# Splitting an output product's and a gate's weights row by row, and an embedding product in three products of parts

## The reference

```python
h = h + jnp.concatenate([att, hm], axis=-1) @ w_out          # "output product", 1024 x 1024
u = rms_norm(h, g_mlp) @ w_ff1                                # 1024 x 4096
h = h + jnp.square(jax.nn.relu(u)) @ w_ff2                    # 4096 x 1024
gate = jax.nn.sigmoid(rms_norm(h, g_ple) @ w_ple_gate + b_ple_gate)
return h + gate * (p_i @ w_ple)                               # p_i: 512 x 256, w_ple: 256 x 1024
```

## Time and profile before

| | |
|---|---|
| runs | 2102.87, 2107.33, 2102.92 us; median 2102.92 |
| profiled execution | 2106.63 us, of which its span 2104.8 us and 1.83 us around it |
| TensorE busy | 2043.9 us, 97% of the span |
| VectorE, ScalarE, GpSimd busy | 1120.6, 864.4, 918.7 us |
| transfers | 194.28 MB, mean 92 GB/s |

### The profile page before, as it was taken

How to read it: one execution, slowest core, us unless ns; L and a number is a source line. 1 busy time by engine, 2 the same in 40 slices (tenths; PEclk the granted TensorE clock), 3 DMA queues, 4 the chain that set the end, 5 groups by cost and what they waited for, 6 DMA issues and landing times.

```text
span 2104.8 us, 26346 instructions
## 1 busy us (share of the span) xinstructions
PE 2043.9 (97%) x10220; PEld 1583.3 (75%) x10220; DVE 1120.6 (53%) x1991; ACT 864.4 (41%) x1373; POOL 918.7 (44%) x1152
## 2 busy tenths in 40 slices
PE   6999999999999999999999999999999999999998
PEld 3877677888888767667888888666766788888867
DVE  5366758986483578944523131446986443123134
ACT  4542434343233557753322222335677432222132
POOL 1344205787575334731655555103455055555530
PEclk9999999999999999999999999999999999999999
DMA  9134631333322310212333322222112133332212
GB/s 320 42 115 143 204 118 41 101 101 100 101 80 87 100 41 21 81 41 81 110 100 100 100 98 83 80 81 66 41 41 81 50 101 101 100 100 84 98 59 100
DMA packets 186668, 194.28 MB, mean 92 GB/s; under 512 B 8496, under 2 KB 181936, under 8 KB 186160
## 3 DMA queue, kind: packets, MB, share of 16 engines
q1 hardware_dynamic: 185968, 189.44, 27.7%
q10 hardware_dynamic: 576, 3.15, 0.4%
HBM read 190.48 MB, written 2.10 MB: 91 GB/s over the span
## 4 chain that ended last, share of the span: by engine, by line
PE 87%; DVE 5%; POOL 3%; ACT 2%; DMA 1%; issue 1%; SPq 0%; ACTq 0%; DVEq 0%; POOLq 0%
PE ps L804 20%; PE ps L806 19%; PE ps L805 19%; PE ps L821 3%; PE ps L823 3%; PE ps L822 3%; PE ps L849 2%; POOL arena_m L2881 2%; PE ps L1256 1%; PE ps L1311 1%; POOL wl L2813 1%; DVE mix L2441 1%; PE ps L1344 1%; PE ps L1363 1%; PE ps L906 1%; PE ps L838 1%
## 5 line engine op out<-in xcount | busy, mean ns | idle before, releaser
L2813 POOL TENSOR_TENSOR wl<-ring,wh 128x256 fp32r<-128x256 f32 x1000 | 748.7, 783 | 853.1 <-ACT wh L1454 852.8
L1454 ACT ACTIVATE wh<-ring 128x1024 fp32r<-128x1024 f32 (+2 forms) x294 | 304.1, 1044 | 326.6 <-PE ps L806 256.2
L804 PE MATMUL ps<-xh,wh 128*128 128x512 f32 (+1 forms) x976 | 383.9, 393 | 3.2 <-POOL wl L2813 2.3
L806 PE MATMUL ps<-xh,wl 128*128 128x512 f32 (+1 forms) x976 | 381.3, 391 | 0.0
L805 PE MATMUL ps<-xl,wh 128*128 128x512 f32 (+1 forms) x976 | 381.2, 391 | 0.0
L804 PE MATMUL ps<-acts,wh 128*128 128x512 f32 x880 | 345.0, 392 | 3.7 <-DVE wl L1974 3.3
L806 PE MATMUL ps<-acts,wl 128*128 128x512 f32 x880 | 342.5, 389 | 0.0
L805 PE MATMUL ps<-acts,wh 128*128 128x512 f32 x880 | 342.4, 389 | 0.0
L2441 DVE SCALAR_TENSOR_TENSOR mix<-ps,par,mix 128x441 f32<-128x441 f32 (+2 forms) x352 | 213.8, 687 | 32.4 <-ACT mix L1685 32.4
L804 PEld LDWEIGHTS ps<-xh,wh 128*128 128x128 f32 (+1 forms) x976 | 183.4, 188 | 48.3 <-issue 9.6
L806 PEld LDWEIGHTS ps<-xh,wl 128*128 128x128 f32 (+1 forms) x976 | 183.3, 188 | 39.3
(11 more groups left out here) (435 smaller groups left out, 3033.1 us busy)
## 6 DMA issues: line engine op xcount, KB each, us to landing
ring<-in_w_ff_dram SPq DMA_DIRECT2D x64, 1024.0 KB, 5.2
ring<-in_w_in_dram SPq DMA_DIRECT2D x28, 1024.0 KB, 5.2
ring<-in_ffn_w_up_dram SPq DMA_DIRECT2D x22, 1024.0 KB, 4.9
ring<-in_w_ada_dram SPq DMA_DIRECT2D x17, 1024.0 KB, 5.0
ring<-in_w_out_dram SPq DMA_DIRECT2D x12, 1024.0 KB, 5.0
ring<-in_ffn_w_down_dram SPq DMA_DIRECT2D x8, 1024.0 KB, 4.9
ring<-in_w_ple_gate_dram SPq DMA_DIRECT2D x8, 1024.0 KB, 5.0
early<-in_w_ada_dram SPq DMA_DIRECT2D x7, 1024.0 KB, 10.7
```

What stands on the lines that cost most here:

```text
L804: t.matmul(b[0:m, 0:n], s.hi[:, k, a:a + m], x2[0][:, k, :], start=k == ks[0], stop=False)
L806: i = t.matmul(b[0:m, 0:n], s.lo[:, k, a:a + m], x2[0][:, k, :], start=False, stop=k == ks[-1])
L1454: a.activation(s.hi[:, :, c], s.ap[:, :, c], ACT.Copy).then_inc(*up("hi", "hi", name, hf))
L2813: i = p.tensor_tensor(s.lo[:, k:k + 2, c], s.ap[:, k:k + 2, c], s.hi[:, k:k + 2, c].bitcast(F32), ALU.subtract)
```

## The change

1. The embedding weights become a split tile: four transfers of 256 x 256 put columns 256 q of `w_ple` at steps 2q and 2q+1 of an ordinary 8-step tile, so that even output rows lie in half 0 and odd ones in half 1. The ring slot is released by the splits.
2. `p_i` is split too, before the last feed-forward product: ACT writes two high rows into `xh`, DVE two low rows into `xl`.
3. Each embedding row is six matmuls of parts instead of two plain ones, in the row order 0, 2, 4, 6, 1, 3, 5, 7. ACT takes out rows 0, 4, 1, 5, DVE rows 2, 6, 3, 7, and the reciprocal stands behind row 6.
4. `part` makes its note at the second step with `ahead` 3, and one with `ahead` 0 at the first. In layer l, ACT calls `high` for rows 1 to 3 of the output product one row earlier than before.
5. For the gates, `high` and `low` of row j+1 are called in row j's turn (row 0's before the loop), and gate row 6 of layer 0 gets a note that holds the last half of the gates' weights.

```diff
-            W.add(("ple", l), A["w_ple_2"][l], 2, 1024, split=False)
+            W.add(("ple", l), [A["w_ple_2"][l][:, q * 256:q * 256 + 256] for q in range(4)], 8, 256)
...
+        PLE_ROWS = (0, 2, 4, 6, 1, 3, 5, 7)
...
-            if name[0] == "ple":
-                return done(("pw", name[1], 7))
...
-                for src in s.srcs:
+                for q, src in enumerate(s.srcs):
                     w = src.shape[1]
-                    d.dma_start(s.ap[:, :, o:o + w], src.rearrange("(k p) n -> p k n", p=128)).then_inc(
-                        *up(f"slot{s.i % NSLOT}", "load", s.name, by=16))
+                    to = s.ap[:, 2 * q:2 * q + 2, :] if s.name[0] == "ple" else s.ap[:, :, o:o + w]
+                    d.dma_start(to, src.rearrange("(k p) n -> p k n", p=128)).then_inc(*up(f"slot{s.i % NSLOT}", "load", s.name, by=16))
...
-                if not second:
-                    use(key, name, (hf,), True, 3 if keep else 0)
+                if second:
+                    use(key, name, (hf,))
+                else:
+                    use(key, name, (hf,), True, 0)
...
-                for j in range(8):
-                    b = take(("pw", l, j))
-                    e.wait_ge(*at("load", s.name))
-                    e.wait_ge(*at("ple", l))
+                for j in PLE_ROWS:
+                    key, q, c = ("pw", l, j), j // 2, slice(128 * (j % 2), 128 * (j % 2) + 128)
+                    use(key, s.name, (j % 2,))
+                    b = take(key)
+                    e.wait_ge(*at("lo", s.name, j % 2))
+                    e.wait_ge(*at("pTl", l))
                     for k in range(2):
-                        i = t.matmul(b[:, :], s.ap[:, k, j * 128:j * 128 + 128], n.pT[:, k, :], start=k == 0, stop=k == 1)
-                    i.then_inc(*full(("pw", l, j)))
+                        t.matmul(b[:, :], s.hi[:, 2 * q + k, c], xh[:, k, :], start=k == 0, stop=False)
+                        t.matmul(b[:, :], s.hi[:, 2 * q + k, c], xl[:, k, :], start=False, stop=False)
+                        i = t.matmul(b[:, :], s.lo[:, 2 * q + k, c], xh[:, k, :], start=False, stop=k == 1)
+                    i.then_inc(*full(key))
...
-                use(("pw", l, 7), s.name, (), ahead=0)
...
                     if l == 0 and j == 6:
+                        use(("pg", l, j), ("pg", l, 3), (1,), False)
                         first_rows(1, range(3))
...
                 for j in range(8):
-                    high(("wo", l, j))
+                    if j >= 4:
+                        high(("wo", l, j))
                     feed(("m", l), j, taken(("wo", l, j)), ("g_mlp_2", l), n.sq2, xh, done(("mo", l, 3)))
+                    if j < 3:
+                        high(("wo", l, j + 1))
...
                 down2(2)
+                e.wait_ge(*at("ple", l))
+                e.wait_ge(*done(("ff1", l, 3, 7)))
+                for k in range(2):
+                    a.activation(xh[:, k, :], n.pT[:, k, :], ACT.Copy).then_inc(*up("act", "pTh", l, k))
                 down2(3)
                 rows_of(("parts", ("p", l)), n.part)
-                out_of(("pw", l, 0), n.pw[:, 0, :])
-                root(("p", l), n.rs2)
-                for j in range(2, 8, 2):
-                    out_of(("pw", l, j), n.pw[:, j, :])
+                for m, j in enumerate(PLE_ROWS):
+                    high(("pw", l, j))
+                    if m % 2 == 0:
+                        out_of(("pw", l, j), n.pw[:, j, :])
+                    if m == 0:
+                        root(("p", l), n.rs2)
+                high(("pg", l, 0))
...
-                    high(("pg", l, j))
+                    if j < 7:
+                        high(("pg", l, j + 1))
...
                 down2(2)
+                for k in range(2):
+                    e.wait_ge(*at("pTh", l, k))
+                    v.tensor_tensor(xl[:, k, :], n.pT[:, k, :], xh[:, k, :].bitcast(F32), ALU.subtract).then_inc(*up("vec", "pTl", l))
                 down2(3)
-                inverse(("p", l), n.rs2)
-                for j in range(1, 8, 2):
-                    e.wait_ge(*done(("pw", l, j)))
-                    v.tensor_copy(n.pw[:, j, :], ps(("pw", l, j))[:, :]).then_inc(*free(("pw", l, j)))
+                for m, j in enumerate(PLE_ROWS):
+                    low(("pw", l, j))
+                    if m % 2:
+                        e.wait_ge(*done(("pw", l, j)))
+                        v.tensor_copy(n.pw[:, j, :], ps(("pw", l, j))[:, :]).then_inc(*free(("pw", l, j)))
+                    if m == 3:
+                        inverse(("p", l), n.rs2)
+                low(("pg", l, 0))
...
-                    low(("pg", l, j))
+                    if j < 7:
+                        low(("pg", l, j + 1))
```

## The result

The changed kernel takes **2087.3 us**, median of 4 executions (2085.3 to 2088.9), beside 2104.3 us of the kernel before in 4 executions on the same chip: ratio 0.9917, 95% interval 0.9900 to 0.9934. The forecast was 2089.4 us with a range of 2086 to 2096. The median is 17.0 us lower, where 13.5 us were forecast; the profiled spans differ by 2104.8 - 2086.3 = 18.5 us.

What follows compares the result with a forecast made beforehand. TensorE, busy 97% of the span, was taken to bound the kernel. Embedding rows 4.9, gates and `tok 0` 6.0, output products 2.4 and first block 0.2 sum to 13.5 us off the 2102.92 us median: 2089.4 us, range 2086.5 to 2096.

Steps and rivals of the forecast that it cites:

- Embedding rows: Embedding stage of both layers: 48 matmuls of parts replace plain ones, gaining 2.7 + 2.2 = 4.9 us, between 0 and 6.0.
- Bank 0: Layer 0, embedding row 3 and gate row 0 share this bank, so TensorE waits 0.5 us before gate row 0.
- Gates and `tok 0`: At `first_rows`: the 4.32 us wait and 1.65 us of slow clock go, 6.0 us; between 4.3 and 6.5, or 0.
- the second rival: Second half of `tok 0` still split after gate row 6; wait and slow clock stay, 2095.4 us; chance 0.06.
- Output products: Row 4's 1.64 us wait goes, leaving about 1.2 us per layer, 2.4 us; first block's 0.22 us wait gives 0.2 us.
- the new wait before the fourth sum of squares: Layers' output products: DVE's 4.3 us per row makes row 3's square late, so TensorE waits 0.4 to 0.5 us.
- the stretch at 1393 us: Behind the `first_rows` stall: 3.30 us at clock 0.50, half of it lost, 1.65 us to be gained.
- The first: Embedding rows: DVE sets the pace, gate row 0 waits in both layers, the 4.9 us are gone, 2094.3 us; chance 0.12.
- third: DVE pacing the embedding rows and the late `tok 0` split both happen, 2100.3 us; chance 0.04.
- fourth: A new stall drops the clock and it stays at 0.50; 45 us of it gives 2112 us; chance 0.03.

## Why the prediction was right, and where it was not

**Embedding rows: right.** Forecast 2.7 + 2.2 = 4.9 us; steps of 2.7 + 2.2, and 5.0 us when the part was taken out. The distance of parts, 0.227 us, held. `fold` between parts cost 11.94 - 10.9 = 1.0 us, a little under the 1.2 of one plain matmul among parts. Bank 0 made the wait, of 0.28 us in the record instead of 0.5; moving the reciprocal removed it. The Trainium skill's figure of 215.7 ns (page "TensorE: Matmul & The Clock Gate", section "Wait — 56ns, not 53.3ns?") would, as an estimate, have put the last embedding matmul 48 x 0.0113 = 0.5 us earlier; the trace, at 0.227 us, does not agree with it here either.

**Gates and `tok 0`: right in sum.** 4.5 + 1.55 = 6.05 us against 6.0. The low part ended 1.2 us ahead, as forecast. Less right was the account of the edit: the text had the note and the order do it together, and the second rival stood on the note. The order does all of it. The slow clock behind this stall was in all four profiles that have the stall, and in none of the ten others, so its 1.65 us were safe to count.

**Output products: the term that was mis-sized.** Forecast 2.4 + 0.2 us, measured 3.5 + 0.4 in one pair of profiles and 3.9 in all in another. Two things. First, a removed wait was priced at its recorded idle time. From matmul start to matmul start the 0.22 us were worth 0.4, the 1.64 us 1.8 to 1.9, the 0.28 us 0.42 and 0.11 more, the 4.32 us 4.5. The rows say why: a matmul record lasts 0.39 us while the next starts 0.23 us behind it, so idle is counted from an end that lies 0.16 us past the point where the next was due; and the first matmul after a wait can have its successor later than 0.23 us behind it (0.34 us at 1342.88 in after, 0.30 at 957.56 in before). Second, the new wait before the fourth sum of squares was forecast at 0.4 to 0.5 us and is at most 1.22 - 1.07 = 0.15: DVE's chain takes 957.57 - 953.48 = 4.09 us for each row, not 4.3, as its adds of rows 2 and 3 show, and ACT's square of row 3 stands right behind. The timelines of DVE and ACT of the kernel after:

```profile
953.48 0.68 DVE L2500 TENSOR_TENSOR h<-h,ps 128x512 f32<-128x512 f32 x1
...
957.57 0.68 DVE L2500 TENSOR_TENSOR h<-h,ps 128x512 f32<-128x512 f32 x1
```

```profile
958.28 0.63 ACT L1479 ACTIVATE arena_f<-h 128x512 f32<-128x512 f32 x1 [1.89 <-DVE h L2500]
```

The square was forecast at 962.2 in the time of the old trace; it ends at 958.91 in the new one, where all stands 2.5 us earlier up to there, thus 0.8 us sooner than forecast.

**The clock: partly open.** The forecast took only the stretch at 1393 us. Of the others, one at 46 to 49 us and one at 1518 to 1533 us stand in all fourteen profiles; the rest come and go with the execution. The Trainium skill says of the start of a kernel (same page, "What's actually happening") that the number of slow matmuls differs from run to run; here it is so in the middle of the run too: spans of the changed kernel's one file were 2083.2, 2086.3 and 2090.9 us with four, five and seven stretches. So the 3.6 us of the profiled pair that stand outside the forecast were luck in good part: eight stretches against five, and the two waits in mixers. Whether the clock's share was luck in whole is not settled. 3.1 us less were lost in the mean, 1.65 of it forecast, which leaves 1.4 us with an error of 0.7. The medians of the four and four executions differ by 17.0 us where 13.5 were forecast: 1.3 of the 3.5 us are the mis-sized term, and most of the rest is luck of a few executions, since over all of them the gain is 15.4 us. The place at 345 us was slow in 3 of 4 profiles with the first block's old splits and in 1 of 8 with the new ones and the same 2.14 us wait there; that points to the timing of the change, but is too few to show it.

**The rivals.** The first, DVE sets the pace of the embedding rows, did not come: it waits for TensorE between copies. Nor did the second, third and fourth; no new stall that repeats was over 0.28 us.

## What to carry to other kernels

Price a TensorE stall from start to start, not by its idle time: here waits of 0.2 to 0.3 us cost nearly twice what is recorded. Before moving work out of the way of a stall, ask which of the pieces ends the wait, and change the order of that one alone; and before shortening one, see whether the engine that feeds the stretch behind it is already busy 95% of the time, as DVE was behind 341 us. Where half-clock stretches differ between executions of one file, compare kernels by medians of many executions and by steps between the same matmuls, not by the difference of two profiled spans.

## What the runs showed that was not expected

- Half-clock stretches stand behind short stalls too. Before 311 us there are two waits of 0.78 and 0.57 us close together, before 345 us one of 2.14, and the granted clock behind the same waits was 0.50 in some executions and 1.00 in others of one file (1.00 at 311 us in two profiles of the changed kernel; a stretch at 0.50 from 312 us on in the third). No run shows what decides it.
- The 4.32 us stall was followed by 0.50 each time, the 1.64 us stalls before row 4 never, in the three profiles that have them.
- A half-clock stretch can cost nothing: the 1.85 us lost in that at 762 us came back as a wait for ACT that was not needed. Taking stretches times 1.65 us overstates what the clock costs.
- 48 matmuls of parts with plain `fold` between them take 11.94 us where 32 records of plain matmuls with the same `fold` take 14.30: for 512 columns a plain product is two records of 0.43 us, three products of parts are 3 x 0.227 = 0.68 us.
